# A ring of 12 slot pairs, turned rows behind the second layer and a later output bias in a decoder layer

## What is computed

```python
h = rms_norm(x, norm1_w)
rq, rk, rv, rg, mq, mk, mv = split(h @ w_in)                 # 1024 x 3072
ret = group_norm(retention(rot(rq), rot(rk), rv)) * ret_norm_w
ret = silu(rg) * ret
moba = softmax_attention(rot(mq), rot(mk), mv)               # causal, one block of 256
x = x + concat(ret, moba) @ w_out                            # 1024 x 1024
h2 = rms_norm(x, norm2_w)
top_logit, top_e = top_k(h2 @ w_router + b_router, 4)
gate = softmax(top_logit)
for e in range(32):                                          # tokens routed to e
    u = h2[tok] @ w1[e] + b1[e]                              # 1024 x 2048
    y = clamped_swiglu(u) @ w2[e] + b2[e]                    # 1024 x 1024
    acc[tok] += y * g
out = rms_norm(x + acc, final_norm_w)
```

## Time and profile before

| | us |
|---|---|
| median of 3 runs | 1079.09 (1077.97 to 1081.16) |
| profiled execution | 1079.07 |
| its span, from the first to the last instruction | 1077.3 |
| TensorE busy | 1031.3 (96%) |
| VectorE busy | 223.5 (21%) |
| ScalarE busy | 115.3 (11%) |
| POOL busy | 2.3 |
| first layers, line 1184 | 450.7 |
| second layers, line 1196 | 227.0 |

### The profile page before, as it was taken

One profiled execution on the slowest core, in us unless ns is written; L12 is line 12 of the kernel. 1 busy time (PEld: TensorE's weight loads), 2 busy tenths in 40 slices (PEclk: granted clock), 3 DMA queues, 4 the chain that ended last, 5 costly groups with the idle time before them and its releaser, 6 DMA issues.

```text
span 1077.3 us, 12049 instructions
## 1 busy us (share of the span) xinstructions
PE 1031.3 (96%) x5013; PEld 424.6 (39%) x5013; DVE 223.5 (21%) x582; ACT 115.3 (11%) x220; POOL 2.3 (0%) x8
## 2 busy tenths in 40 slices
PE   8999999999999999999999999989999999999995
PEld 7888653333333333333333333323333333333332
DVE  1264432111111111111111111111111111111112
ACT  1131120000000000000000000000000000000002
POOL 0000000000000000000000000000000000000000
PEclk9999999999999999999999999989999999999999
DMA  9982568999999999999999999999999999999994
GB/s 315 369 344 79 200 283 334 431 426 428 427 428 426 427 427 429 427 428 427 427 427 428 428 428 426 427 426 428 428 428 427 428 428 427 428 427 427 428 428 168
DMA packets 45231, 424.71 MB, mean 394 GB/s; under 512 B 5840, under 2 KB 18384, under 8 KB 20592
## 3 DMA queue, kind: packets, MB, share of 16 engines
q1 hardware_dynamic: 42224, 422.07, 93.7%
q10 hardware_dynamic: 2720, 1.12, 0.4%
q0 software_dynamic: 224, 0.66, 0.2%
HBM read 422.78 MB, written 1.05 MB: 393 GB/s over the span
## 4 chain that ended last, share of the span: by engine, by line
PE 89%; DMA 5%; ACT 2%; DVE 2%; issue 1%; SPq 0%; DVEq 0%; ACTq 0%
PE PS L1184 39%; PE PS L1196 20%; PE PS L939 7%; PE PS L1170 5%; PE PS L1144 5%; DMA ring<-in_w 4%; PE PS L1153 3%; PE PS L1055 3%; PE PS L1233 2%; PE PS L1162 2%; ACT late L515 2%; PE PS L1131 1%; DMA ring<-in_w_in 1%; PE PS L1136 0%; PE PS L1252 0%
## 5 line engine op out<-in xcount | busy, mean ns | idle before, releaser
L1184 PE MATMUL PS<-ring,work 128*64 128x512 f32 x2048 | 450.7, 598 | 4.0 <-issue 4.0
L1184 PEld LDWEIGHTS PS<-ring,work 128*64 128x64 f32 x2048 | 145.8, 138 | 286.4 <-issue 286.1
L1196 PE MATMUL PS<-ring,work 128*64 128x512 f32 x1024 | 227.0, 595 | 2.5 <-DMA ring<-in_w 2.5
L1196 PEld LDWEIGHTS PS<-ring,work 128*64 128x64 f32 x1024 | 70.8, 137 | 135.2 <-issue 129.5
L819 DVE TENSOR_SCALAR work<-PS 128x512 f32<-128x512 f32 x32 | 22.1, 692 | 398.8 <-PE PS L1184 398.8
L939 PE MATMUL PS<-ring 128*128 128x256 f32 x384 | 86.7, 385 | 3.0 <-DMA ring<-in_w_in 3.0
L803 DVE COPY work<-PS 128x256 f32<-128x256 f32 x32 | 13.6, 425 | 318.7 <-PE PS L1131 318.7
L939 PEld LDWEIGHTS PS<-ring 128*128 128x128 f32 x384 | 73.1, 193 | 14.3 <-DMA ring<-in_w_in 3.1
L510 ACT ACTIVATE work<-work 128x512 f32<-128x512 f32 x32 | 20.2, 630 | 532.4 <-DVE work L819 532.4
L1170 PE MATMUL PS<-late,work 64*128 64x512 f32 x256 | 63.6, 615 | 0.8 <-ACT late L515 0.8
L1144 PE MATMUL PS<-resid,work 128*64 128x512 f32 x248 | 58.5, 592 | 0.0
(11 more groups left out here) (152 smaller groups left out, 366.6 us busy)
## 6 DMA issues: line engine op xcount, KB each, us to landing
ring<-in_w SPq DMA_DIRECT2D x192, 2048.0 KB, 29.1
ring<-in_w_in SPq DMA_DIRECT2D x12, 1024.0 KB, 12.0
ring<-in_w_out SPq DMA_DIRECT2D x4, 1024.0 KB, 12.1
resid<-in_x SPq DMA_DIRECT2D x2, 512.0 KB, 4.3
out<-resid SPq DMA_DIRECT2D x4, 256.0 KB, 2.0
ring<-in_consts ACTq DMA_DIRECT2D x1, 800.0 KB, 9.4
ring<-in_final_norm_w SPq DMA_DIRECT2D x1, 512.0 KB, 38.7
work<-in_b POOLq DMA_DIRECT2D x3, 128.0 KB, 7.4
```

The source lines that it names most:

```text
L1184: last = mm(bank(v)[64 * half:64 * half + 64, :], gh[:, c, :], ring[:, 2 * d + c % 2, v * F + half * BANK:v * F + (half + 1) * BANK], star ...
L1196: last = mm(bank(5)[64 * half:64 * half + 64, :], aT[:, c, 64 * h:64 * h + 64], ring[:, 2 * d + c // 2, cols:cols + BANK], start=(h == 0 a ...
```

## The change

The ring gets 24 slots, 12 pairs, so load g waits for slice g - 12, and twelve loads are issued in the head, with number 11 right behind number 10. `probT` and `retw` move into slot 22, `work` shrinks by 256 columns, and the scratch that is kept for descriptors of POOL's DMAs is set to 1024 bytes; POOL issues no DMA any more. SP issues b1 and b2, ahead of load 11, which waits for the new semaphore `gated` (VectorE's last read of `retw`). ScalarE's queue issues the load of `retw` at the start. `gx` is no longer `late` but `g_sb`, so that ScalarE's copy of the rows must wait for the sigmoid and for VectorE's product, which read `g_sb`. The turn stands behind the second layer instead of ahead of it. The accumulators are opened by the combine of step 1, and the output bias is added behind the combine of step 3 (`BIAS_STEP`). The steps are 7 unrolled, two rounds of 12, and the last one.

```diff
-SLOTS_1M = 22
+SLOTS_1M = 24
...
-PEEL = 9
-UNROLL = 11
+PEEL = 7
+UNROLL = 12
...
+BIAS_STEP = 3
...
+DGE_SCRATCH = 1024
...
-FIRST_ORDER = [0, 1, 2, 3, 4, 5, 10, 6, 8, 7, 9]
+FIRST_ORDER = [0, 1, 2, 3, 4, 5, 10, 11, 6, 8, 7, 9]
...
-        work = sb("work", [P, 12 * SEQ + 4 * 3 * P])
+        work = sb("work", [P, 12 * SEQ + 5 * SEQ])
...
-        probT = work[:, 3840:4608].rearrange("p (s n) -> p s n", s=2)
+        probT = ring[:, HEAD_CHUNKS + 6, 0:768].rearrange("p (s n) -> p s n", s=2)
         decayed = prob
-        retw = nat[:, 0, MQ:MQ + 512]
+        retw = ring[:, HEAD_CHUNKS + 6, 768:1280]
...
-        gx = late[:, :]
+        gx = g_sb
...
                 if g == 10:
                     sp.wait_ge(decayed_ready, RET_HEADS)
                     sp.wait_ge(chunk_used, WIN_CHUNKS)
+                elif g == 11:
+                    sp.wait_ge(probT_ready, MOBA_HEADS)
+                    sp.wait_ge(pv_done, 4)
+                    sp.wait_ge(ret_done, RET_HEADS)
+                    for v in range(2):
+                        sp.dma_start(b1_sb[v * E:(v + 1) * E, :], b1[0, :, v * F:(v + 1) * F]).then_inc(late_in, 16)
+                    sp.dma_start(b2_sb, b2[0, :, :]).then_inc(late_in, 16)
+                    sp.wait_ge(gated, T)
...
-        @block.gpsimd
-        def _(pool):
-            pool.wait_ge(qkT_done, 4)
-            pool.dma_start(retw, ret_norm_w.broadcast_to([P, 512])).then_inc(retw_in, 16)
-
-            pool.wait_ge(probT_ready, MOBA_HEADS)
-            pool.wait_ge(pv_done, 4)
-            pool.wait_ge(ret_done, RET_HEADS)
-            for v in range(2):
-                pool.dma_start(b1_sb[v * E:(v + 1) * E, :], b1[0, :, v * F:(v + 1) * F]).then_inc(late_in, 16)
-            pool.dma_start(b2_sb, b2[0, :, :]).then_inc(late_in, 16)
-            pool.wait_ge(late_in, 48)
...
+            act.dma_start(retw, ret_norm_w.broadcast_to([P, 512])).then_inc(retw_in, 16)
             act.dma_start(brb, b_router.broadcast_to([P, E])).then_inc(small_in, 16)
...
             def take_rows(n):
 
+                act.wait_ge(sig_ready, n)
+                act.wait_ge(glin_ready, n)
                 act.wait_ge(rows_done, n)
...
-                link(nc.vector.tensor_tensor(nat[:, t, RG:RG + 512], nat[:, t, RG:RG + 512], retw, ALU.mult))
+                ins = nc.vector.tensor_tensor(nat[:, t, RG:RG + 512], nat[:, t, RG:RG + 512], retw, ALU.mult)
+                ins.then_inc(gated, 1)
+            dve.wait_ge(gated, T)
...
-            def combine(n):
+            def combine(n, start=False):
...
-                                  start=False, stop=False, skip_group_check=True)
+                                  start=start, stop=False, skip_group_check=True)
...
                     bias(n + 1)
-                    turn_rows(n + 1)
-                if first:
-                    start_accumulators()
                 if j > 0:
                     pe.wait_ge(actT_ready, n)
                     down(r, i, j)
+                if j < LAST:
+                    turn_rows(n + 1)
                 pe.wait_ge(act_ready, n + 1)
...
                 if j > 0:
-                    combine(n)
+                    if isinstance(r, int) and j == 1:
+                        pe.wait_ge(gatesT_ready, 1)
+                    combine(n, isinstance(r, int) and j == 1)
+                if isinstance(r, int) and j == BIAS_STEP:
+                    add_down_bias()
...
-            def start_accumulators():
+            def add_down_bias():
...
-                           start=True, stop=False, skip_group_check=True)
+                           start=False, stop=False, skip_group_check=True)
```

More of the change, by code:

```diff
@@ L246, in layer_kernel @@
         retw_in = sem("retw_in")
+        gated = sem("gated")
         late_in = sem("late_in")
@@ L1307 @@
     from concourse.bass_utils import run_bass_kernel_spmd
-    nc = bacc.Bacc("TRN2", target_bir_lowering=False, num_devices=1)
+    nc = bacc.Bacc("TRN2", target_bir_lowering=False, num_devices=1, dynamic_dma_scratch_size=DGE_SCRATCH)
     arrays, args = {}, []
```

## The result

| | before | changed |
|---|---|---|
| median, us | 1079.09 (5 runs, 1077.14 to 1081.16) | 1069.97 (5 runs, 1068.55 to 1070.98) |
| profiled execution, us | 1079.07 | 1070.12 |
| its span, us | 1077.3 | 1068.3 |
| TensorE's waits for expert loads, us | 2.5 | 12.1 |

The changed kernel takes 0.9912 of the time, with a 95% interval of 0.9894 to 0.9931: 9.1 us less by the medians, 9.0 by the two profiled executions. The forecast was 7.9.

The account below looks back on a forecast made before the run. The load stream was taken as the bound, TensorE's path 2.5 us behind: load 190 at 1044.0 instead of 1051.9, plus a 25.4 us tail, gives span 1069.4, plus 1.8 makes 1071.2 us; range 1069.0 to 1075.5.

Parts of the forecast that it names:

- The two bounds: Load stream and TensorE's own path, within 2.5 us of each other; the stream ends later, and a change must move both.
- Part 1: Twelfth slot pair in the head, its load issued at about 119.5 into an idle DMA stretch: -4.94 us.
- Part 2: Output bias moved from step 0 to step 3: load 17 lands at 189.9, DMA hole closed, -3.0 us.
- Part 3: Turn behind the second layer: 27.43 us a step, -20.4 us of TensorE's path, none showing directly, 5.4 needed.
- Part 4: Small edits: gate weight's queue 0, between -0.6 and +0.6 us; loop's jump back, 6.9 us, hidden by 14 us spare.
- The sum: Load 190 lands at 1044.0, plus tail of 25.4: span 1069.4; plus 1.8: 1071.2 us.
- (a): Only the slot counts, the hole at 185 in step 0 stays: 1074.1 us; chance 0.10.
- (b): TensorE's path isn't shortened, it keeps 28.1 us a step: 1076.6 us; chance 0.06.
- (c): Clock falls mildly, one drop a step in the six starved last steps: 4 us, 1075; chance 0.05.
- (d): Slower than before, clock drops twice in a step: 21 us over 6 steps, 1092; chance 0.04.

Follow-up runs that it names:

- the first of the loaded kernels: Changed kernel with half of the gather done twice in every step but the last: 1108.23 us, ratio 1.027.

## Why the prediction was right, and where its sizes were off

**The two bounds.** Right. Turn alone: no gain and 18.6 us of waits; slot pair and bias without the turn: the loads 9.9 us earlier and the end only 5.4 us in the two traces.

**Part 1.** Right to 0.1 us: issued at 119.4 (119.5 forecast), in the empty stretch, and the stream a whole interval ahead. It pushed load 7 by 1.4 us (landing at 140.1 and not at 138.7) and the next, load 9, by 0.2; by then the delay was used up. The idle stretch behind load 10, which the prediction had as a reserve, wasn't needed: it is empty from 157 to 161.3 before and after. The prediction's 158.8 is the landing of the last load; the rate was zero from 157 on.

**Part 2.** Load 17 at 189.9, as forecast. Step 1 began at 176.9 and not at 177.3, and its first slot came free at 180.5 and not at 182.0, since the fall of the clock that the earlier trace rows contain (15.02 for a first layer of 13.88) didn't come here. The load didn't land earlier for it: the queue was the later of the two, as the step had it.

**Part 3.** Right: 27.43 us a step. That the 20.4 us would show as nothing directly is what the turn alone showed; that 5.4 of them would be needed, slot pair and bias, with 4.5.

**Part 4.** The jump back cost TensorE about 7 us and was hidden. Spare time 14 us forecast, 12.1 and 9.9 found by the waits of two executions, 12.8 and 14.8 by adding work. That the small edits cost nothing at the head fits the first refill, at 161.3 and before at 161.4; no run takes them apart. Starvation began in step 26, so in the last six steps, as forecast.

**The sum.** 1069.4 forecast as span, 1068.3 measured. Load 190 landed 1.1 us earlier than summed: 173 intervals of 4.931 and not 4.937 give 1.0. So about 1 us of the gain belongs to none of the parts, and it is nearly all that the forecast missed in the span. The ring's depth isn't its cause, since the two kernels with 11 pairs and the later bias have 4.930 too. Single intervals of 5 to 6.5 us stand in all traces (one of 7.4 in the first of the loaded kernels), at different places; what interrupts the stream there is open.

**Rivals.** (a) would have been 1074.1; the combination that keeps the hole, slot pair and turn, ran at 1072.5. (b) would have been 1076.6; its test, slot pair and bias, gave 1074.9. In both the price was 1.6 or 1.7 us too high, likely for the reason of the slot pair alone: TensorE's path and the head move by 1 to 3 us with falls of the clock from one execution to the next. In the trace of slot pair and turn, for one, step 0 had no fall, and load 17 landed at 184.2 + 7.7 = 191.9 where the old kernel's number 16 landed at 192.9. (c) and (d), the clock in the starved stretch: the waits of the changed kernel left it at 1.00.

```profile
884.00:1044.00 160.00, 147.26 (x688) 49.03 (x690) 26.34 (x56) 12.74 (x21) 0.00 (x0) 1.00 1.01 428
```

That is 92% busy, with waits of up to 2.56 us. In one of the eleven other traces, bias and turn, the clock did fall there, for 3.4 us behind a wait of 2.8 us. The Trainium skill (TensorE: Matmul & The Clock Gate, HAM oscillation — how this bites in real kernels) speaks of bursts shorter than the waits between them; here the bursts are longer than the waits, and of the waits in these two stretches only the longest was followed by what it describes.

## What to carry to other kernels

An engine that is 96% busy can be free of charge: compare its period with that of its supply over the whole run, since a full ring at the start hides a supply that is 5% too slow until the last step. Where two bounds lie close together, what an edit shows depends on its company: here the turn showed nothing alone and 4.9 us on top of the other two, and those two, 4.9 and 4.2 us alone, showed only 3.3 together without it. Try such edits in company before dropping one. For a stream that is saturated to the end, look for its holes before saturation and for the event that starts the chain, and take the spare time of the other engine from a run that loads it, with the price of the load read from its own trace.

## What the runs showed of the hardware

**An issue that takes 4 us.** With many loads under way, SP's DMA instruction itself becomes long. The issues from 820 to 1020, in the changed kernel, in the one before and in the turn alone (duration in ns: shortest, median, longest):

```profile
L359 SPq DMA_DIRECT2D ring<-in_w x24: 332/4032/11373, 822.5 to 980.9; - x24
```

```profile
L356 SPq DMA_DIRECT2D ring<-in_w x26: 327/333/1159, 821.4 to 996.6; - x26
```

```profile
L356 SPq DMA_DIRECT2D ring<-in_w x25: 333/3821/6480, 814.3 to 991.9; - x25
```

The third has the ring of 11 pairs, so it isn't the ring's depth. Counted from the issues and landings of the changed kernel, an issue took 0.33 us with up to eight other loads of 2 MB on the way, 1.5 by the median with nine and 4.0 with ten. What holds it isn't shown. The stream doesn't lose by it (426 to 429 GB/s in these slices).

**A fall of the clock without idle time.** The granted clock fell behind the output bias, 32-row matmuls followed by transposes, with TensorE busy all the time. With the bias in step 0 this was so in three of four traces, between 174 and 183; with the bias in step 3 never there, but in five of nine between 260 and 273. The turn alone, slot pair and turn, and, at step 3, slot pair and bias:

```profile
175.00:182.00 7.00, 7.00 (x19) 3.20 (x19) 1.88 (x7) 0.60 (x1) 0.00 (x0) 0.52 0.88 375
```

```profile
175.00:182.00 7.00, 6.70 (x29) 3.22 (x28) 2.26 (x8) 0.69 (x2) 0.00 (x0) 1.00 1.01 433
```

```profile
260.00:268.00 8.00, 8.00 (x24) 2.69 (x24) 1.48 (x6) 0.00 (x0) 0.00 (x0) 0.79 1.00 424
```

A 0.52 is the lower of the two levels, 1.2 GHz, in nearly all of the window.

**Two column halves at the price of one.** In the chain above, four matmuls into both 64-column halves took 1.72 us, two into one half 1.71: leaving one half out of such work would gain nothing.
